# Latent attention with keys and values per head, its masks on GpSimd, its meta keys eight heads at a time

## What is computed

```python
def indexed_sparse_mla(q_abs, c_kv, iq, ik, iw, w_uv, bias_table):
    ...
        _, sel = lax.top_k(score, topk)                      # index scores pick the keys of a query
        valid = (sel <= qpos[None, :, None]) & (sel >= PAD)
        c_sel = gather(c_kv, sel)
        s = jnp.einsum('bqhc,bqkc->bqhk', qa, c_sel).astype(jnp.float32) * scale
        s = jnp.where(valid[:, :, None, :], s + jnp.moveaxis(bias, -1, 2).astype(jnp.float32), NEG)
        pr = jax.nn.softmax(s, axis=-1)
        return jnp.einsum('bqhk,bqkc->bqhc', pr.astype(c_kv.dtype), c_sel)
    ...
    o = jnp.einsum('bphc,chd->bphd', lat, w_uv)
# caller: q_abs = jnp.einsum('bphd,chd->bphc', q, w_uk[l])
```

## Time and profile before

| | |
|---|---|
| three executions, us | 1612.05, 1610.47, 1612.25; median 1612.05 |
| profiled execution, us | 1613.14 |
| its span, us | 1611.4 |
| TensorE busy | 1560.9 us, 97% of the span |
| VectorE, ScalarE, GpSimd busy | 52%, 33%, 13% |
| granted TensorE clock, mean over the span | 0.992 |

### The profile page before, as it was taken

One profiled execution on the slowest core, in us unless ns is written; L12 is line 12 of the kernel. 1 busy time (PEld: TensorE's weight loads), 2 busy tenths in 40 slices (PEclk: granted clock), 3 DMA queues, 4 the chain that ended last, 5 costly groups with the idle time before them and its releaser, 6 DMA issues.

```text
span 1611.4 us, 21667 instructions
## 1 busy us (share of the span) xinstructions
PE 1560.9 (97%) x7682; PEld 1269.9 (79%) x7682; DVE 843.9 (52%) x1500; ACT 536.7 (33%) x994; POOL 204.1 (13%) x142
## 2 busy tenths in 40 slices
PE   7889999999999999999999999999999999999997
PEld 6767886877878888888689777888777888888876
DVE  5378895446555345435664283332665543553454
ACT  4114443533422222222431164444333221221233
POOL 2222220012000000000001462222300000000000
PEclk9999999999999999999999999999999999999999
DMA  5832220013323333323233301211233333333322
GB/s 146 206 98 66 76 62 14 1 33 105 97 87 92 102 91 91 101 84 99 69 92 91 79 2 53 66 53 34 72 104 92 91 104 91 92 92 104 91 79 91
DMA packets 250763, 132.62 MB, mean 82 GB/s; under 512 B 21193, under 2 KB 247621, under 8 KB 250702
## 3 DMA queue, kind: packets, MB, share of 16 engines
q1 hardware_dynamic: 248574, 123.92, 26.9%
q0 software_dynamic: 2048, 7.77, 1.8%
q10 hardware_dynamic: 80, 0.14, 0.0%
HBM read 129.67 MB, written 6.38 MB: 84 GB/s over the span
## 4 chain that ended last, share of the span: by engine, by line
PE 85%; DVE 8%; issue 2%; DMA 2%; ACT 2%; POOL 1%; SPq 0%; DVEq 0%; ACTq 0%; POOLq 0%
PE psL L1577 58%; PE psL L1699 9%; PE psS L1577 5%; PE psL L1819 2%; PE psT L1710 1%; PE psS L1950 1%; PE psS L1797 1%; DMA stage<-in_w_in 1%; DVE acc L1188 1%; DMA xin<-in_x 1%; DVE st L1187 1%; PE psT L1713 1%; DVE wl L922 1%; PE psS L1749 1%; POOL biasD L578 1%
## 5 line engine op out<-in xcount | busy, mean ns | idle before, releaser
L1577 PE MATMUL psL<-hn,wh 128*128 128x512 f32 x1664 | 526.4, 397 | 5.0 <-POOL wl L528 4.6
L1577 PEld LDWEIGHTS psL<-hn,wh 128*128 128x128 f32 x1664 | 313.8, 189 | 83.2 <-POOL wl L528 5.5
L619 ACT ACTIVATE wh<-stage 128x1024 fp32r<-128x1024 f32 (+3 forms) x250 | 243.3, 973 | 346.3 <-PE psL L1577 238.7
L1577 PE MATMUL psL<-hn,wl 128*128 128x512 f32 x832 | 330.6, 397 | 0.0
L922 DVE TENSOR_TENSOR wl<-stage,wh 128x1024 fp32r<-128x1024 f32 (+1 forms) x168 | 201.5, 1199 | 91.2 <-ACT wh L619 87.2
L1577 PE MATMUL psL<-hid,wh 128*128 128x512 f32 x704 | 222.4, 397 | 4.8 <-DVE wl L922 4.8
L528 POOL TENSOR_TENSOR wl<-stage,wh 128x1024 fp32r<-128x1024 f32 (+2 forms) x82 | 156.7, 1911 | 479.9 <-ACT wh L619 479.9
L1577 PEld LDWEIGHTS psL<-hn,wl 128*128 128x128 f32 x832 | 156.8, 188 | 36.5
L1699 PE MATMUL psL<-hn,wh 128*128 128x512 f32 x512 | 179.5, 432 | 1.9 <-DVE tmp L1177 1.7
L1577 PEld LDWEIGHTS psL<-hid,wh 128*128 128x128 f32 x704 | 131.0, 188 | 40.6 <-DVE wl L922 5.9
L1577 PE MATMUL psL<-hid,wl 128*128 128x512 f32 x352 | 139.1, 395 | 0.0
(11 more groups left out here) (368 smaller groups left out, 2007.4 us busy)
## 6 DMA issues: line engine op xcount, KB each, us to landing
stage<-in_w_in SPq DMA_DIRECT2D x54, 512.0 KB, 3.9
stage<-in_w_ffn_gate SPq DMA_DIRECT2D x22, 512.0 KB, 3.8
stage<-in_w_ffn_up SPq DMA_DIRECT2D x22, 512.0 KB, 3.8
stage<-in_w_ff_gate SPq DMA_DIRECT2D x22, 512.0 KB, 3.8
stage<-in_w_ff_up SPq DMA_DIRECT2D x22, 512.0 KB, 3.8
stage<-in_w_out SPq DMA_DIRECT2D x16, 512.0 KB, 3.7
stage<-in_w_ffn_down SPq DMA_DIRECT2D x16, 512.0 KB, 3.7
stage<-in_w_ff_down SPq DMA_DIRECT2D x16, 512.0 KB, 3.7
```

What stands on the lines that cost most here:

```text
L619: act.activation(wh[:, b, 0:n], stage[:, b, 0:n], ACT.Copy).then_inc(hi[b], 1)
L1577: ins = pe.matmul(dst, w[:, b, k * P:(k + 1) * P], x[:, part, k, c0:c1], start=k + n == 0, stop=k == kc - 1 and n == 2)
```

## The change

- **Keys per head.** The queries are no longer taken into the latent space. Four products (`head_keys`, two heads each, 528 columns) make keys per head from `wuk` and `cT`. They go into `kz`, 128 partitions by 8 heads by 528, in which a head has its 64 partitions and the other 64 are zero; VectorE copies the even heads, ScalarE the odd ones, GpSimd writes the zeros. The transposes of `wuk` and `wukT` are gone. `qT` now carries the scale.
- **Values per head.** Five products (`head_values`) make `vB`, 128 keys by 512 (8 heads of 64) for each of the four chunks, and `vM` for the meta keys: 16 meta keys of 8 heads on 128 partitions, masked with `mine8` so that each head meets its own.
- **Mask.** GpSimd adds `selm` to `biasB` for each unit into one of three tiles `biasM` (`mask_bias`); VectorE's `biased` reads `biasM`. The mask's product is gone. GpSimd's `low` for the first weight of `br1` now stands behind all 32 masks.
- **Meta keys.** VectorE copies the 16 meta columns of each unit into `m8`; after eight heads they take one turn: one transpose, one copy, one product of 512 columns.
- **Products with the values** are 64 columns wide, i+1 a unit, and write the output at once; `lat`, its copy and the `wuv` product are gone.
- **Two banks.** Turn n transposes into bank n % 2 of `psT` and waits for the copy of turn n-2, where it was the one before.

```diff
+def stacked_turns():
+    for u in range(NB * NH):
+        yield u, u, u // NH
+        if u and u % NH == 0:
+            yield u, None, u // NH - 1
+    yield NB * NH, None, NB - 1
...
+            pool.wait_ge(key_taken, 1)
+            pool.tensor_copy(cm8[:], cT[:, 0:META].unsqueeze(1).broadcast_to([P, NH, META])).then_inc(cm8_ok, 1)
             lows("gates1")
+            def mask_bias(j):
+                i, h, K, _ = la_units[j]
+                pool.wait_ge(sel_ok, i + 1)
+                if j >= 3:
+                    pool.wait_ge(ph["la"]["neg"], j - 2)
+                pool.tensor_tensor(biasM[:, j % 3, 0:K], biasB[:, h, NKEY - K:NKEY], selm[:, i, 0:K], ALU.add).then_inc(biasM_ok, 1)
+            for b in range(2):
+                pool.wait_ge(mm[b], PAIR0["br1"])
...
+                pool.memset(kz[other, :, :].rearrange("p (c g) k -> p c g k", g=2)[:, :, g, :], 0.0).then_inc(kz_zero, 1)
...
             lows("br1")
...
+            def take_turn(p, n, width, dst):
+                act.wait_ge(p["pt"], n + 1)
+                if n >= 2:
+                    act.wait_ge(p["pv"], n - 1)
+                act.activation(dst[:, n % 2, 0:width], psT[:, n % 2, 0:width], ACT.Copy).then_inc(p["ptx"], 1)
...
-                if j >= 2:
-                    take_pt(p, j - 2, units[j - 2][3], PT[:, j % 2, :])
+                for n, u, i in turns_at(j - 2):
+                    take_turn(p, n, P if u is None else P * len(units[u][3]), PT)
...
-            v.tensor_copy(wukT[:], psS[:, 2, :].rearrange("p (c f) -> p c f", c=4)).then_inc(key_taken, 1)
...
+            def even_keys(c):
+                v.wait_ge(kz_mm, c + 1)
+                v.tensor_copy(as_halves(kz[0:HD, 2 * c, :], NKEY), kz_banks(c)[0:HD, :, 0:NKEY // 2]).then_inc(kz_even, 1)
...
+            v.tensor_tensor(vM[:].rearrange("p (h d) -> p h d", h=NH), vB_bank(NB).rearrange("p (h d) -> p h d", h=NH),
+                            spread(mine8[:], HD), ALU.mult).then_inc(vB_d, 1)
...
+                v.tensor_copy(m8[:, i % 2, h * META:(h + 1) * META], cols).then_inc(p["meta"], 1)
...
                     v.wait_ge(p["s"], j + 1)
+                    v.wait_ge(biasM_ok, j + 1)
...
-                    v.tensor_copy(lat[:, u % 2, :], psL[:, 0, 0:P]).then_inc(p["lat"], 1)
...
+            def head_keys(c):
+                if c == 0:
+                    for b in range(2):
+                        pe.wait_ge(ev[b], PAIR0["br1"])
+                elif c == 1:
+                    pe.wait_ge(ph["w1"]["ptx"], NB * NH)
                 else:
+                    pe.wait_ge(kz_even, c - 1)
+                    pe.wait_ge(kz_odd, c - 1)
...
-                        pe.matmul(dst, q, cT[:, k0:k1], start=True, stop=False)
-                        ins = pe.matmul(dst, identb[:], selm[:, i, k0:k1], start=False, stop=True)
+                        ins = pe.matmul(psS[:, 2 * (j % 2) + bank, 0:k1 - k0], q, kz[:, h, k0:k1], start=True, stop=True)
...
+                for n, u, i in turns_at(j - 3):
+                    pe.wait_ge(p["ptx"], n + 1)
+                    if u is None:
+                        pe.matmul(psL[:, i % 2, :], PT[:, n % 2, 0:P], vM[:], start=False, stop=True, skip_group_check=True).then_inc(p["pv"], 1)
+                        continue
...
+                        ins = pe.matmul(psL[:, i % 2, h * HD:(h + 1) * HD], PT[:, n % 2, m * P:(m + 1) * P], vB[:, c, h * HD:(h + 1) * HD],
+                                        start=h == 0 and m == 0, stop=m == i, skip_group_check=True)
```

More of the change, by code:

```diff
@@ L238, in build @@
         wuv = keep("wuv", [P, NH * HD])
-        wukT = keep("wukT", [P, 4, P])
+        wuk = keep("wuk", [P, NH * HD])
+        cm8 = keep("cm8", [P, NH, META])
+        mine8 = keep("mine8", [P, NH])
         metaT = keep("metaT", [P, 2, KD, META])
@@ L1660, in _ @@
                     pe.transpose(psS[:, n, c * P:(c + 1) * P], src[:, c, :], ident[:])
[L1661 to L1664 removed]
+                ins = pe.transpose(psT[:, 0, n * META:(n + 1) * META], src[0:META, MC, :], ident[0:META, 0:META])
             ins.then_inc(key_t, 1)
@@ L1765, in _ @@
                     ins.then_inc(p["pv"], 1)
-            def absorbed(h):
-                r = slice(h % 2 * HD, h % 2 * HD + HD)
-                if h < 2:
-                    pe.wait_ge(ev[h], PAIR0["br1"])
-                else:
-                    pe.wait_ge(qabs_ok, h - 1)
-                pe.matmul(psL[:, h % 2, :], wukT[r, h // 2, :], qT[r, h // 2, :], start=True, stop=True).then_inc(qabs_mm, 1)
-            absorbed(0)
-            heads_out(0, on, p["on"], (1, 3, 3, 4), lambda i: absorbed(i + 1))
@@ L1777, in _ @@
-            for h in range(NB + 1, NH):
-                absorbed(h)
-            pe.wait_ge(sel_ok, NB)
+            def head_keys(c):
[4 more added lines that the diff above has]
+                    pe.wait_ge(ph["w1"]["ptx"], NB * NH)
+                else:
+                    pe.wait_ge(kz_even, c - 1)
+                    pe.wait_ge(kz_odd, c - 1)
+                for half in range(2):
+                    ins = pe.matmul(kz_banks(c)[:, half, 0:NKEY // 2], wuk[:, c * P:(c + 1) * P], cT[:, half * NKEY // 2:(half + 1) * NKEY // 2],
+                                    start=True, stop=True)
+                ins.then_inc(kz_mm, 1)
@@ new lines, in head_values @@
+            def head_values(c):
+                if c == NB:
+                    pe.wait_ge(cm8_ok, 1)
+                    pe.wait_ge(vB_d, 1)
+                elif c == 0:
+                    pe.wait_ge(kz_even, 3)
+                    pe.wait_ge(kz_odd, 3)
+                elif c == 2:
+                    pe.wait_ge(kz_even, 4)
+                    pe.wait_ge(kz_odd, 4)
+                rows = cm8[:].rearrange("p h m -> p (h m)") if c == NB else cT[:, META + c * P:META + (c + 1) * P]
+                pe.matmul(vB_bank(c), rows, wuv[:], start=True, stop=True).then_inc(vB_mm, 1)
@@ new lines, in _, with turned @@
+            pe.wait_ge(wuk_in, 32)
+            head_keys(0)
+            head_keys(1)
+            heads_out(0, on, p["on"], (1, 3, 3, 4), lambda i: head_keys({1: 2, 3: 3}[i]) if i % 2 else None)
+            for c in range(NB + 1):
+                head_values(c)
+            pe.wait_ge(sel_ok, NB)
+            pe.wait_ge(kz_zero, 2)
+            def turned(p, n, tile, cols):
+                if n >= 2:
+                    pe.wait_ge(p["ptx"], n - 1)
+                for m, col in enumerate(cols):
+                    ins = pe.transpose(psT[:, n % 2, m * P:(m + 1) * P], tile[:, col:col + P], ident[:])
+                ins.then_inc(p["pt"], 1)
@@ L1781, in _ @@
             units = list(latent_units())
             p = ph["la"]
-            for j in range(len(units) + 5):
+            for j in range(len(units) + 4):
                 if j < len(units):
```

160 lines of the change are left out of this document (95 added, 65 removed).

## The result

| | before | changed |
|---|---|---|
| median, us | 1611.26 (1608.94 to 1612.25, 4 runs) | 1585.86 (1581.39 to 1589.87, 4 runs) |
| profiled execution, us; its span | 1613.14; 1611.4 | 1589.87; 1588.1 |
| TensorE busy, mean granted clock | 1560.9, 0.992 | 1538.6, 0.992 |

The ratio is 0.9844, 95% interval 0.9814 to 0.9874. The same kernel measured again (`r1_same`) gave 0.9822 (0.9806 to 0.9838).

What follows compares the result with a forecast made beforehand. In the stage it took ScalarE's order to bind blocks 0 to 2 and TensorE's work block 3. 1613.14 - 16.0 - 0.6 + 0.1 gave 1596.6 profiled, 1.1 above the median: 1595.5 us, range 1589 to 1602.

Steps and rivals of the forecast that it cites:

- 1613.14 - 16.0 - 0.6 + 0.1: Profiled execution before, less the latent attention stage, less the `wukT` copy, plus the stretch ahead of the stage: 1596.6 us.
- The loop after the change: Latent attention: the wait over VectorE and ScalarE sets steps of 1.24, 1.48, 1.71 in blocks 0 to 2, 1.95 in block 3.
- TensorE's work: Latent attention: scores, transposes and value products sum to 0.56, 1.08, 1.61, 2.13 us a step, binding in block 3 alone.
- The check that was to guard this step: Old block 0: 276.63 - 274.80 = 1.83, less 0.40 ahead of the transposes, is the 1.43 between score starts.
- Of which the 0.4 that TensorE waits in a step hides nearly half: Block 1 of latent attention: the meta keys' 0.11 + 0.87 us is nearly half hidden by TensorE's wait in a step.
- The stage: First latent attention scores to the transposes of `heads_out`: 58.1 us against 74.1, so -16.0.
- Ahead of the stage: Stretch before latent attention: 1.0 us more work but hardly any waits, between -0.3 and +1.5, taken as +0.1; zeros cost nothing.
- `wukT`: Where the index keys are taken: its copy, last in front of `key_taken`, goes and TensorE waits less, -0.6 us.
- The index scores 0.6 earlier: Sign expected in the profile after: the index scores start 0.6 us earlier.
- the loop doesn't bind: Rival in latent attention: TensorE's work binds in all blocks because ScalarE gets ahead; 6.7 us less, 1588.8; chance 0.13.
- VectorE is held: Rival in latent attention: GpSimd's masks hold VectorE's copy of the meta columns; +2 us, 1597.5; chance 0.14.
- A dear mask: Rival in latent attention: GpSimd masks at twice the 512 row exceed the steps of blocks 2 and 3; 1604.7; chance 0.07.

Runs made afterwards that it cites:

- r1_shift: The kernel before with 544 unused bytes per partition, so later tiles lie where they lie in the changed kernel: 1609.24 us, ratio 0.9956.
- r2_pad32: The kernel before with 8 unused float32 words (32 bytes) behind `wukT`: 1606.72 us, ratio 0.9966.
- r3_after_pad32: The changed kernel with 32 unused bytes behind `subg`, so `gate`, `hn`, `mix` and `hid` start 32 bytes behind a multiple of 64: 1590.96 us, ratio 0.9854.
- r1_copy_first: The changed kernel with ScalarE's copies of unit j-2 ahead of its exponential of unit j: 1579.66 us, ratio 0.9777, stage 50.0.
- r2_old_copy_first: The kernel before with ScalarE's copies of unit j-2 ahead of its exponential of unit j in the latent attention: 1610.36 us, ratio 0.9976.
- r4_hn_only: The kernel before with 32 unused bytes in front of `hn` and 32 more before `mix` and `hid`, moving only `hn` onto a multiple of 64: 1609.46 us.
- r4_mix_only: The kernel before with 32 unused bytes in front of `mix` and `hid`, which then start on a multiple of 64: 1609.78 us, ratio 0.9975.
- r3_mask_twice: The changed kernel with each GpSimd mask computed twice, one behind the other: 1589.36 us, ratio 0.9843, stage 58.7.

## Why the prediction was wrong

Two steps failed, and both made the forecast too long. **The larger one is a term that the sum put at nothing without a word**: "1613.14 - 16.0 - 0.6 + 0.1" carries everything outside the change over as it was. But the change's new tensors moved `gate`, `hn`, `mix` and `hid` by 544 bytes, and the products over them ran faster: 5.0 us in the four stretches shown, 5 to 8 us for the kernel (`r1_shift`, `r2_pad32`, `r3_after_pad32`). Most of the 9.6 us by which the median was missed comes from here.

**The step that failed inside the stage** is "The loop after the change": "Ahead of the value products in a step stand scores and transpose, 0.36. Step: 1.24." It closed the loop over one step. But the value products that wait for ScalarE stand in TensorE's next step, and it is the scores of the step after that which they hold up: scores j, exponential j, copy j-2, values j-2, scores j+2. The period is half of passage and values. With the prediction's own passages, 1.60 to 3.28, and 0.2 to 0.8 of values, that is 0.90, 1.28, 1.66 and 2.04, where it had 1.24, 1.48, 1.71 and 1.95; measured were 0.92, about 1.3, 1.7 and 2.2 (the last is TensorE's work). `r1_copy_first`, which cuts the loop, shows that it was there. The check that was to guard this step was none: it took the distance from scores to the next transposes and subtracted what stands between, which gives the distance of the scores again, whatever the loop. The old kernel would have tested it: the passage of 1.83 and 0.86 of work behind it, halved, are 1.35, and 1.32 to 1.43 were there. It would have been a weak test, since in `r2_old_copy_first` these steps still take 1.32.

Point by point:

- **TensorE's work** 0.56, 1.08, 1.61, 2.13: right. `r1_copy_first` ran at 0.6, 1.12, 1.67, 2.2. The value product's 0.2 held as well (three in 0.62, from 305.03 to 305.65), not the 25 ns that the table of the Trainium skill has for up to 64 columns (TensorE: Matmul & The Clock Gate, Back-to-back issue gap).
- **Blocks 0 to 2** were 1.4, 1.1 and 0.0 shorter than forecast. The right loop would have given about 4 less over the three; the meta turns took back 1.5. "Of which the 0.4 that TensorE waits in a step hides nearly half" was wrong: they cost their full 0.98 and some 0.5 more, since ScalarE's second copy and the big product lie in the loop. Block 3 and tail: 23.4, forecast 23.0.
- **The stage**: 56.0, forecast 58.1. It came this near because two errors partly cancelled, the loop and the meta turns. This is 2.1 of what was missing, 9.6 us by the medians and 6.7 in the profiled executions.
- **Ahead of the stage**: right, and by its mechanism. Forecast was +0.1 with 0.4 for the wait for both `psL` banks; at like clock it is +0.1, with 0.48 for that wait. The zeros cost nothing, as forecast.
- **`wukT`**: TensorE's wait shrank from 3.10 to 2.40, -0.7 where -0.6 was forecast. "The index scores 0.6 earlier" can't be read off: the mark moves by 6 us between profiles.
- **The clock outside the stage** was taken as fixed too. In the profiled executions it gave 3.0 us between index scores and stage, and took 3.4 behind 905 us, where `r3_mask_twice` without that low stretch needs 1261.7 for the rest of the program and the changed kernel 1265.0. The low stretch at 252 us shows in five of seven profiles with the old attention (not in `r4_hn_only` and `r4_mix_only`) and in none of nine with the new, and in the same five the index scores run low for longer. The old attention runs with it and without it. Whether the new one only happened to escape it, and what decides it, stays open, and with it up to 3 us of the difference of the medians.
- **The rivals**: "the loop doesn't bind" gave 6.7 less for the stage's sum and is refuted for this kernel, yet the total came out nearer to it, for other reasons. "VectorE is held" is refuted for the reason given, and its mechanism is real (`r3_mask_twice`). The Trainium skill (GPSIMD Engine Reference, Key points) states that GpSimd shares its SBUF interfaces with VectorE and contends with some of its instructions; the copy of 0.99 us agrees. A dear mask and a slow clock in the stage did not occur.

## What to carry to other kernels

When engines wait for each other in a staggered loop, write the loop down with the index of each step, count how many steps it spans, and test it on the old kernel with a number that isn't in the derivation. An in-order engine should first empty what another one waits for and then start its long instruction: swapping two statements of ScalarE's list was worth a third of what the whole change gave in its stage. And when an edit changes the size of a tensor, compare the start of every tensor behind it, because products that the edit doesn't touch may change their rate.

## What the runs showed of the hardware

- A product stream over `mix` takes 51.3 to 51.4 us for 219 instructions when `mix` starts 32 bytes behind a multiple of 64 (counted from the first tensor), and 50.5 when it starts on one (1.7%); over `hn` and `hid` it is 324.1 to 325.2 and 323.6 us for 1392 (0.2 to 0.5%), over `hn` alone 49.21 to 49.24 and 49.14 to 49.17 us for 405 (0.1 to 0.2%). For the whole kernel that is 5 to 8 us.
- A VectorE copy from SBUF to SBUF that starts during a two-input GpSimd instruction ends 0.03 us behind it, 24 times in `r3_mask_twice`, up to 1.04 us in place of 0.17; the GpSimd instruction is not slowed (1.19). GpSimd adds a float32 and a bfloat16 tensor in 1191 ns for 528 columns, less than it needs for 512 of its other two-input group (1332).
- After the same wait for `selm`, 1.5 to 1.7 us, TensorE ran at 0.50 for some 3.4 us in five profiles and at 1.00 in eleven. The same five took 18.7 us from the index scores to the window attention, the others 17.2 to 17.3.
